# Reordering the first four weight tiles of every stage in a two-block transformer-like kernel

## The reference, cut to what matters

```python
# first block: root-mean-square norms
hn = rms_norm(h, norm_mix[layer])
h = h + mixer(hn, ...)            # layer 0: retention and gated delta rule; layer 1: gated linear recurrence
h = h + conv_ffn(rms_norm(h, norm_ffn[layer]), w_up, ..., w_down)
# second block: layer norms, after each sum
x = layer_norm(alpha * x + 0.5 * swiglu(x, ffn_w_gu[l, 0], ffn_w_down[l, 0]))
x = layer_norm(alpha * x + token_mixers(x, w_in[l], ...))
x = layer_norm(alpha * x + 0.5 * swiglu(x, ffn_w_gu[l, 1], ffn_w_down[l, 1]))
```

## Time and profile before

| | |
|---|---|
| median of 3 runs | 3392.9 us (3392.31 to 3396.19) |
| the profiled execution | 3396.75 us, span 3395.0 us |
| granted TensorE clock, mean | 0.984 of full |
| TensorE matmul busy | 3264.5 us (96%) |
| VectorE busy | 2229.3 us (66%) |
| ScalarE busy | 1578.9 us (47%) |
| DMA | 285.82 MB, mean 84 GB/s |

### The profile page before, as it was taken

How to read it: one execution, slowest core, us unless ns; L and a number is a source line. 1 busy time by engine, 2 the same in 40 slices (tenths; PEclk the granted TensorE clock), 3 DMA queues, 4 the chain that set the end, 5 groups by cost and what they waited for, 6 DMA issues and landing times.

```text
span 3395.0 us, 50953 instructions
## 1 busy us (share of the span) xinstructions
PE 3264.5 (96%) x20848; PEld 2827.0 (83%) x20848; DVE 2229.3 (66%) x3238; ACT 1578.9 (47%) x2501; POOL 16.8 (0%) x21
## 2 busy tenths in 40 slices
PE   7999999999999999999999989999999999989998
PEld 6888888888888888999866689998999875688997
DVE  6672666448666537767686577677677667676776
ACT  5324344337444325434466454355444457654443
POOL 0000000001000000000000000000000000000000
PEclk9999999999999999999999999999999999999999
DMA  3211223232232222322211123222222211022222
GB/s 132 81 45 50 98 96 99 97 98 93 75 101 97 98 89 85 117 103 95 74 44 40 38 72 115 100 89 86 100 99 101 75 63 46 14 87 99 95 106 75
DMA packets 82942, 285.82 MB, mean 84 GB/s; under 512 B 9264, under 2 KB 11312, under 8 KB 82224
## 3 DMA queue, kind: packets, MB, share of 16 engines
q1 hardware_dynamic: 81952, 279.08, 24.1%
q0 software_dynamic: 784, 3.80, 0.4%
HBM read 278.66 MB, written 2.10 MB: 83 GB/s over the span
## 4 chain that ended last, share of the span: by engine, by line
PE 84%; DVE 10%; ACT 3%; issue 2%; DMA 1%; DVEq 0%; ACTq 0%
PE gb L767 14%; PE gb L768 13%; PE gb L769 13%; PE gb L979 7%; PE gb L981 7%; PE gb L980 7%; PE pm L767 4%; PE pm L768 4%; PE pm L769 4%; PE gb L1539 2%; DVE wl L2457 2%; PE pm L1576 1%; PE pm L1556 1%; DVE rinv L2487 1%; DVE work_a L3376 1%
## 5 line engine op out<-in xcount | busy, mean ns | idle before, releaser
L767 PE MATMUL gb<-xh,wh 128*128 128x512 f32 (+1 forms) x1952 | 723.9, 371 | 61.7 <-DVE xl L2513 37.6
L768 PE MATMUL gb<-xl,wh 128*128 128x512 f32 (+1 forms) x1952 | 700.4, 359 | 0.0
L769 PE MATMUL gb<-xh,wl 128*128 128x512 f32 (+1 forms) x1952 | 700.2, 359 | 0.0
L2457 DVE TENSOR_TENSOR wl<-wst,wh 128x1024 fp32r<-128x1024 f32 (+3 forms) x396 | 444.8, 1142 | 252.8 <-ACT wh L1699 250.3
L1699 ACT CAST wh<-wst 128x1024 fp32r<-128x1024 f32 (+3 forms) x396 | 379.5, 981 | 443.4 <-DMA wst<-in_weights 443.3
L767 PEld LDWEIGHTS gb<-xh,wh 128*128 128x128 f32 x1952 | 381.7, 196 | 151.6 <-issue 51.5
L768 PEld LDWEIGHTS gb<-xl,wh 128*128 128x128 f32 x1952 | 382.6, 196 | 51.3 <-issue 4.8
L769 PEld LDWEIGHTS gb<-xh,wl 128*128 128x128 f32 x1952 | 382.1, 196 | 51.3
L979 PE MATMUL gb<-hid,wh 128*128 128x256 f32 x912 | 258.4, 283 | 3.5 <-DVE wl L2760 3.5
L767 PE MATMUL gb<-hid,wh 128*128 128x512 f32 (+1 forms) x732 | 257.0, 351 | 2.7 <-DVE wl L2457 1.2
L979 PE MATMUL gb<-xh,hid 128*128 128x256 f32 x912 | 258.2, 283 | 0.0
(11 more groups left out here) (475 smaller groups left out, 6334.8 us busy)
## 6 DMA issues: line engine op xcount, KB each, us to landing
wst<-in_weights SPq DMA_DIRECT2D x300, 512.0 KB, 3.3
work_a<-in_weights SPq DMA_DIRECT2D x152, 512.0 KB, 4.1
wst<-in_weights SPq DMA_DIRECT2D x62, 384.0 KB, 3.0
wst<-in_weights SPq DMA_DIRECT2D x28, 320.0 KB, 3.0
h<-in_x_t SPq DMA_DIRECT2D x2, 1024.0 KB, 6.3
work_a<-work_a POOLq DMA_DIRECT2D x8, 256.0 KB, 3.5
out_t<-h SPq DMA_DIRECT2D x8, 256.0 KB, 2.2
tab<-in_first SPq DMA_DIRECT2D x1, 1760.0 KB, 14.7
```

Source lines behind the costliest of these rows:

```text
L767: pe.matmul(dst, w_hi, x_hi, start=start, stop=False)
L768: pe.matmul(dst, w_hi, x_lo, start=False, stop=False)
L769: return pe.matmul(dst, w_lo, x_hi, start=False, stop=stop)
L2457: dve.tensor_tensor(wl[:, s, m, a], wst[:, s, m, a], f32(wh[:, s, m, a]), ALU.subtract).then_inc(lo_split, 1)
```

## The change

Only the order of the 32 pieces in `two_by_half` changes; the pieces themselves, the waits inside them and the signals they raise stay as they are. In the first token half, the second tile's piece comes right behind the first tile's piece for every input pair. In the second token half, the first three tiles go together, pair by pair, and the fourth tile follows alone.

```diff
-                together = (0, 0), (0, 1), (1, 0), (0, 2), (1, 1), (0, 3), (1, 2), (1, 3)
-                for v in range(2):
-                    for m, j in sorted(together) if v else together:
-                        two_tiles(v, 0, m, j)
-                        if v == 0 and m == 0 and j == 3 :
+                for j in range(KT // 2):
+                    for m in range(2):
+                        two_tiles(0, 0, m, j)
+                        if m == 0 and j == 3:
                             sums(n, ln_run, 1)
-                    for m in range(2):
-                        for j in range(KT // 2):
-                            two_tiles(v, 1, m, j)
+                for m in range(2):
+                    for j in range(KT // 2):
+                        two_tiles(0, 1, m, j)
+                for j in range(KT // 2):
+                    for tile in range(3):
+                        two_tiles(1, tile // 2, tile % 2, j)
+                for j in range(KT // 2):
+                    two_tiles(1, 1, 1, j)
```

## The result

The changed kernel takes 3412.93 us (median, 3410.53 to 3415.45); the kernel before, run beside it, 3395.26 us (3392.31 to 3396.19). The ratio is 1.0055, with a 95% interval of 1.004 to 1.007: 17.7 us slower, against 17.6 forecast. The time lies in the range, and in the likeliest case's own range of 3403 to 3418.

What follows compares the result with a forecast made beforehand. TensorE was taken to bound the kernel, with 84% of the chain that ended last. Moved starts of 7.4 us plus clock loss of 10.2 made 17.6, on 3392.9 giving 3410.5 us; range 3396 to 3419.

Steps and rivals of the forecast that it cites:

- likeliest case: Whole kernel: the forecast of 3410.5 us with its own range of 3403 to 3418 us, chance 0.55.
- Waits for the pairs: Starts of the ten stages: TensorE's waits for pieces of the normed input fall from 53.1 to about 35 us.
- Feed-forwards of the first block: Two stages: chunk 2 starts 3.6 us later in each, as its load, cast and the evictions hang on `half_done`; +7.2 us.
- Grouped and token-mixer stages: Six stages: starts of chunk 2 move -0.8 us (grouped) and -0.4 us (mixers); TensorE's earlier arrival becomes waiting.
- if chunk 2 starts earlier in the grouped stages: Grouped feed-forwards: one of two stated signs that the forecast is wrong; the other was ScalarE evicting before its cast.
- So the sums come when they did: First token half, all ten stages: the added piece lies in a 2.93 us wait, so feature sums don't move.
- Norm runs ahead: Rival, layer-norm stages: clock stays up, second halves end 0.7 to 1.5 us sooner, about -6 to -8 us; chance 0.15.
- Sum of the moved starts: First term: starts of chunk 2 over all stages, 7.2 + 1.7 - 0.3 - 0.4 - 0.8 = +7.4 us.
- first mixer: First mixer's chunk 2: 4.0 us of slack against a 3.6 us delay, so it starts 0.3 us earlier.
- recurrence: Linear recurrence's chunk 2: taps end 2.6 us later, weights follow, so it starts 1.7 us later.
- The second term, the clock: Ahead of chunk 2: nine waits, six charged 1.7 us of slowed matmuls each, +10.2 us; bounds 0 and 15.3.
- upper end of the range: Whole kernel: 3419 us, from 22.7 us plus some 3 for closely spaced loads sharing the DMA engines.

Runs made afterwards that it cites:

- evict-first run: Changed kernel, but in the first block's two feed-forwards ScalarE evicts chunk 0 before casting chunk 2, and VectorE adds taps before its subtraction: 3402.74 us, ratio 1.0023.
- second half alone: Kernel before with the new order of the second token half only, the first half in its old order: 3425.93 us, ratio 1.0099.
- old second half in two stages: Changed kernel with the old order of the second token half in the first block's two feed-forwards alone: 3403.87 us, ratio 1.0025.
- only two tiles together: Changed kernel, but in the second token half only chunk 0's two tiles alternate by pair and chunk 1's follow one after the other: 3393.61 us, ratio 0.9998.

## Why the prediction was right in the number and wrong in its split

- **Waits for the pairs**, as forecast. 53.1 fell to 36.7 us where about 35 was forecast. In the stage of the earlier trace rows the waits in the second half are gone.
- **Feed-forwards of the first block, +3.6 us each.** Measured +2.7 and +2.2. The mechanism was the one named: in the second feed-forward the load of chunk 2 issues 3.0 us later against the stage's start (937.27 - 915.43 against 930.86 - 912.04; 3.6 forecast), ScalarE is idle 8.92 us ahead of the cast (6.13 before, near 10 forecast), TensorE's wait 4.34 us (0.83 before, about 5 forecast); the evict-first run removes it. Without the new first half the delay is 4.1 and 4.6, next to the 4.3 of the forecast. What was too small is what comes off it: I took one piece, 0.72 us, and the changed first half gives 1.4 and 2.4. In the second feed-forward 0.6 us of the missing 1.4 are the earlier sums, and 0.8 the time from the load's issue to the cast, 3.30 us where it had been 4.10.
- **Grouped and token-mixer stages.** Right in that nothing starts later and that TensorE's head start turned into waits of 4.42 and 4.87 us (4.4 and 3.6 forecast). But my own sign of being wrong, "if chunk 2 starts earlier in the grouped stages", came true: it starts 1.8, 0.3, 0.5 and 0.7 us earlier against the stage's start, where I had 0, 0, 0 and 0.8. Forecast -1.2 us in sum for the six, measured -4.8.
- **The step that failed**, first of two terms: *"So the sums come when they did"*. They came 0.54 us earlier against their stage's start in the stage of the earlier trace rows, since the clock stayed up. That was the mechanism of the rival *Norm runs ahead*, which I held to be too weak because "the filler is only 0.7 us long". It was long enough in six stages: the clock there reads 1.00 up to the sums. The sums came 0.3 to 1.9 us earlier in nine of the ten stages. Sum of the moved starts: forecast +7.4, measured -0.7, with the first mixer at -1.3 for -0.3 and the recurrence at +0.4 for +1.7. Stage by stage this error follows the sums: it is 1.0 us in the first mixer (sums 1.0 earlier), 0.9 in the first feed-forward (0.9), 1.3 in the recurrence (1.3), and 1.8, 0.3, 0.5 and -0.1 in the four grouped stages (1.9, 0.3, 0.5 and 0.0); the second feed-forward is told above. The token mixers took up less than their sums gave (0.5 and 0.6 of 1.7).
- **The second term, the clock**: forecast 10.2 us with a bound of 15.3, measured 19.4 by the stages, and 16.3 to 17.6 by the run with unread matmuls. The price of 1.7 us was read behind waits of 2.77 us and shorter; the new waits are mostly 4 to 5 us, and eight of the ten stages lose 1.4 to 4.2 us behind them. In the grouped stages it is 1.7, 2.5, 2.8 and 3.0. With one wait in three uncharged I was wrong too: only the recurrence, with the shortest of these waits (2.26 us), gave nearly nothing (+0.2). That wait is no safe one, though: in three other runs (second half alone, evictions first, old second half in two stages) the recurrence waited 2.27 us and the clock read 0.72 to 0.74 over the next 6 us, at a cost of 1.6 to 1.8 us. With only two tiles together a wait of 2.26 us was followed by 0.72 and waits of 2.32, 2.56 and twice 2.77 us by 1.00. Bound and price both came from waits that were not like the new ones.
- The two errors, -8.1 and +9.2 us, nearly cancel. Late signals and a low clock behind the new waits were both at work as named, but neither term had its size, and that 17.6 us met the measured 17.7 is luck.
- The 3 us at the upper end of the range, for loads that share the DMA engines, rest on no row, and no run prices them; the one load read above took 3.30 us to its cast, less than before.

The pattern that the Trainium skill describes (TensorE: Matmul & The Clock Gate, the section on HAM oscillation) has waits of some 3 to 5 us for a transfer, each with a throttled burst behind it. This agrees with the trace: seven of the nine waits here are that long, 4.12 us and more, though for VectorE's results and not for a transfer, and behind all seven the clock fell. Of the two shorter ones, 2.38 and 2.26 us, it fell behind the first as well. The section also prices throttled time at half of its length; where TensorE is busy throughout, the trace agrees (6.00 us at 0.50, and +2.79 us behind chunk 2). Over the whole execution it misleads here, for the mean granted clock is the same while the time is 18.7 us longer: what counts is how much work lies in the slow stretches.

The other rule of the Trainium skill that I weighed (DMA: Bandwidth & Descriptors, rules for kernel authors) is to issue early and wait late; I had priced the later issues, counted in full, at 21.3 us. The trace doesn't bear that out: in the six grouped and token-mixer stages chunk 2 starts no later, and in the others at most 2.7 us.

Open: why the second token-mixer stage loses 4.2 us behind chunk 2 and the first 2.2, and why the two halves together cost less than their sum. For the first, single executions scatter that much: with waits of at most 1.5 us ahead of chunk 2 (seven of the runs above) the part behind it in these two stages still lay between 3.0 us below and 1.7 above the kernel before. The stages are read from one execution of each kernel, and each low stretch's place is that execution's; the sums agree with the medians within a few us, a single cell may not.

## What to carry to other kernels

A wait of the engine that bounds the kernel costs more than its length if a dense stretch of matmuls follows it: in the stage of the earlier trace rows, 2.0 us of waiting in three portions and 0.9 us behind them were cheaper than one wait of 4.4 us ahead of dense work. Before putting work early to close small waits, ask where its signals stood (here 6 pieces behind the first tile's end where 12 had been) and where the waiting goes. And when two terms of a sum both hang on the clock, price them together: here one piece more in a wait kept it up, and the longer waits that the same change made let it fall further on.

## What the runs showed of the hardware

Matmuls that nobody reads made the kernel faster: 14 or 28 of them in each of nine waits of 2.3 to 4.9 us took 17.6 us off the changed kernel, and up to 14 in each stage's first wait took 7.1 us off the kernel before. A little real work can do the same: in the stage of the earlier trace rows two pieces, 12 matmuls, ahead of the first wait where there had been one held the granted clock at 1.00 for the next 10 us, where with one piece it read 0.78, 0.50 and 0.72 in the same three stretches, changing between 2.4 and 1.2 GHz. Up to the feature sums it read 1.00 in six of the nine stages in which it had been low; in the other three it still fell.

The same wait does not always cost the same. In the trace of the second half alone, a wait of 3.41 us ahead of chunk 2 was followed by 6 us at a granted clock of 0.54 in the second grouped stage, and one of 3.42 us by 6 us at 1.00 in the last.
